# The convolution group's GLU projection inside the attention stream of a hybrid decoder block

## The reference

```python
h = rms_norm(x, norm_mix[l])
z = h @ w_in[l]                                               # (B,T,IN_WIDTH)
q, kc, vc, ksl, vsl, kw, vw, g, u = jnp.split(z, splits, axis=-1)
...
o_cmp, p_cmp = compressed_attention(q, k_cmp, v_cmp, slopes)
# selected-block branch (top-k blocks from compressed scores)
sel_idx = select_blocks(p_cmp, T)
o_slc = selected_attention(q, rms_norm(ksl.reshape(kv_shape), k_norm_slc[l]), vsl.reshape(kv_shape), sel_idx, slopes)
# sliding-window branch
o_win = window_attention(q, rms_norm(kw.reshape(kv_shape), k_norm_win[l]), vw.reshape(kv_shape), slopes)
gates = jax.nn.sigmoid(g + gate_b[l]).reshape(B, T, G, Hg, N_BRANCH)
o_nsa = (gates[..., 0:1] * o_cmp + gates[..., 1:2] * o_slc + gates[..., 2:3] * o_win).reshape(B, T, NSA_WIDTH)
# Conformer convolution group
o_conv = conformer_conv(u, conv_w[l], conv_b[l], conv_ln_g[l], conv_ln_b[l])
x = x + jnp.concatenate([o_nsa, o_conv], axis=-1) @ w_out[l]
```

## Time and profile before

| | us |
|---|---|
| median of 3 runs | 2215.68 (2213.09 to 2215.70) |
| the profiled execution | 2215.39 |
| its span, slowest core (3) | 2214.3 |
| spans of the eight cores | 2204.7 to 2214.3 |
| TensorE busy, core 3 | 1892.4 |
| VectorE, ScalarE, GpSimd busy | 993.2, 496.4, 126.6 |

### The profile page before, as it was taken

How to read it: one execution, slowest core, us unless ns; L and a number is a source line. 1 busy time by engine, 2 the same in 40 slices (tenths; PEclk the granted TensorE clock), 3 DMA queues, 4 the chain that set the end, 5 groups by cost and what they waited for, 6 DMA issues and landing times.

```text
span 2214.3 us, 30692 instructions; the slowest of 8 cores (2204.7 to 2214.3 us)
## 1 busy us (share of the span) xinstructions
PE 1892.4 (85%) x11010; PEld 999.1 (45%) x11010; DVE 993.2 (45%) x1726; ACT 496.4 (22%) x951; POOL 126.6 (6%) x129
## 2 busy tenths in 40 slices
PE   4898879976666779929957679999999999999999
PEld 2555534443334534318843344444444444444444
DVE  3565591014666666843257634144144144134134
ACT  3222221014776852230033210000000000000000
POOL 1100100100000000001000000010010010010000
PEclk9999999976878999959969879999999999999999
DMA  9621963653210200029622202852852852862853
GB/s 217 121 77 24 110 72 44 66 68 55 40 30 1 40 1 1 1 82 206 95 39 39 38 7 33 113 80 37 113 79 38 112 81 38 111 82 38 110 77 152
DMA packets 187219, 153.20 MB, mean 69 GB/s; under 512 B 12992, under 2 KB 176448, under 8 KB 182720
## 3 DMA queue, kind: packets, MB, share of 16 engines
q0 software_dynamic: 173968, 107.13, 38.1%
q1 hardware_dynamic: 13104, 44.12, 6.4%
HBM read 249.83 MB, written 8.52 MB: 117 GB/s over the span
## 4 chain that ended last, share of the span: by engine, by line
PE 78%; DVE 11%; issue 3%; another core or an unknown queue 3%; ACT 3%; POOL 1%; DMA 0%; DVEq 0%; ACTq 0%; SPq 0%; POOLq 0%
PE bank L1139 14%; PE bank L1156 14%; PE bank L1141 14%; PE bank L470 13%; PE bank L1020 5%; PE bank L949 5%; PE bank L730 3%; PE bank L709 2%; PE bank L477 2%; DVE arena L421 2%; DVE arena L457 1%; PE bank L417 1%; PE bank L1106 1%; PE bank L647 1%
## 5 line engine op out<-in xcount | busy, mean ns | idle before, releaser
L470 PE MATMUL bank<-arena 128*128 128x512 bf16 (+2 forms) x1728 | 329.9, 349 | 10.2 <-DVE arena L614 6.7
L1139 PE MATMUL bank<-arena 128*128 128x512 bf16 x1408 | 319.8, 380 | 0.0
L1141 PE MATMUL bank<-arena 128*128 128x512 bf16 x1408 | 318.3, 379 | 0.0
L1144 DVE TENSOR_TENSOR arena<-bank,arena 128x512 bf16<-128x512 f32 x88 | 60.8, 691 | 548.4 <-PE bank L1139 442.8
L1156 PE MATMUL bank<-arena 128*128 128x512 bf16 x1408 | 305.7, 379 | 0.0
L1159 DVE TENSOR_TENSOR arena<-bank,arena 128x512 f32<-128x512 f32 x352 | 242.4, 691 | 60.7 <-DVE arena L1159 37.7
L1143 ACT ACTIVATE arena<-bank 128x512 bf16<-128x512 f32 x88 | 52.5, 597 | 824.0 <-PE bank L1139 810.8
L470 PEld LDWEIGHTS bank<-arena 128*128 128x128 bf16 x1728 | 152.1, 99 | 177.8 <-issue 16.1
L719 ACT ACTIVATE arena<-bank,arena 128x512 bf16<-128x512 f32 (+2 forms) x504 | 213.5, 530 | 59.5 <-PE bank L709 24.2
L1139 PEld LDWEIGHTS bank<-arena 128*128 128x128 bf16 x1408 | 138.2, 98 | 167.0 <-issue 1.9
L1141 PEld LDWEIGHTS bank<-arena 128*128 128x128 bf16 x1408 | 137.8, 98 | 166.1
(11 more groups left out here) (124 smaller groups left out, 1326.3 us busy)
## 6 DMA issues: line engine op xcount, KB each, us to landing
arena<-xc SPq DMA_DIRECT2D x24, 1024.0 KB, 9.3
arena<-w_gate POOLq DMA_DIRECT2D x22, 1024.0 KB, 14.7
arena<-w_up POOLq DMA_DIRECT2D x22, 1024.0 KB, 16.7
arena<-w_down POOLq DMA_DIRECT2D x22, 1024.0 KB, 13.4
arena<-w_in POOLq DMA_DIRECT2D x18, 1024.0 KB, 13.2
arena<-w_out POOLq DMA_DIRECT2D x8, 1024.0 KB, 32.6
y<-arena SPq DMA_DIRECT2D x8, 1024.0 KB, 3.9
arena<-sel SPq DMA_DIRECT2D x4, 1024.0 KB, 8.1
```

The source lines that it names most:

```text
L470: op(PE, lambda: nc.tensor.matmul(bank[psi][:, 0:n], lhsT=wt[:, kc, cc * 128:(cc + 1) * 128], rhs=actT[:, kc, t0:t0 + n], start=(kc == 0), ...
L1139: op(PE, lambda: nc.tensor.matmul(bank[pg][:, :], lhsT=wgt[:, kc, cc * 128:(cc + 1) * 128], rhs=h3T[:, kc, tc * 512:(tc + 1) * 512], start ...
L1141: op(PE, lambda: nc.tensor.matmul(bank[pu][:, :], lhsT=wut[:, kc, cc * 128:(cc + 1) * 128], rhs=h3T[:, kc, tc * 512:(tc + 1) * 512], start ...
```

## The change

The stage `u_proj` ahead of the compression is gone. Its matmuls become a generator of single matmuls (three segments of 352 columns instead of 32 + 512 + 512), which a new `run_stream` uses as filler. While the program is built, every engine has a clock (`Eng.clk`): each instruction advances it by `_cost`, and its result is ready after `LATENCY`. At each step `run_stream` takes what can start first on TensorE: a transpose, the next score (up to six tiles ahead; seven `Pt` buffers) or the next value products; if by the clocks TensorE would wait, it issues one matmul of the filler first. A wait on an engine's own earlier result is not charged (`if tok.eng is not self`), and a DMA is charged 3 us.

Banks 6 and 7 now belong to the projection; scores and transposes share banks 0 and 1. The groups no longer overlap: cmp, win and sel of one group, then the next; mask, accumulator and importances are single, the latter two tracked by quarter. The heads' outputs overwrite the queries (`catA = qnT`). The sigmoid becomes 0.5 (tanh(x/2) + 1), its factor 0.5 going into the convolution weights, and `CHUNK` is 256 in head 0 and 512 in the others. The normalised inputs stay in one tile `hT` until the attention ends. The memory stage gets a loop of its own, in the same order as before.

```diff
-CHUNK = [128, 256] + [512] * 6
+CHUNK = [256] + [512] * 7
+NPTS = 7
...
+LATENCY = {"pe": 250.0, "act": 280.0, "dve": 200.0, "pool": 200.0, "sp": 0.0}
+
+def _cost(name, ins):
...
+    if name == "pe":
+        return max(n, 64) / 2.4
+    if name == "act":
...
+        return n / 1.2 + fixed
...
+        return n / (1.92 if small else 0.96) + 68.0
...
+        if tok.eng is not self:
+            self.at = max(self.at, tok.t)
...
+        self.clk = max(self.clk, self.at) + _cost(self.name, ins)
+        self.at = 0.0
+        return Tok(self.sem, self.cnt, self, self.clk + LATENCY[self.name])
...
+        tok = Tok(owner.dsem, owner.dcnt, None, Q.clk + 3000.0)
...
-        for j4 in range(4):
-            wa, wab = wget()
-            wbt, wbb = wget()
...
-                    pa = proj_fm(wa, wab, cc, actT, actb, t0, n)
-                    pb = proj_fm(wbt, wbb, cc, actT, actb, t0, n)
...
-        rot_S = Rot([0, 1, 6])
+        rot_S = Rot([0, 1])
...
-                        at(4, tr)
+                        when([ocbb[oj]], tr)
...
+                        for kc in range(16):
+                            op(PE, lambda: nc.tensor.matmul(bank[6][:, 0:352], lhsT=wbt[:, kc, cc * 128:(cc + 1) * 128], rhs=hT[:, kc, c0:c0 + 352], start=(kc == 0), stop=(kc == 15)), r=[wbb] + hseg[seg], w=[bankb[6]])
+                            yield True
+                        j = rot_sg.next()
+                        op(ACT, lambda: nc.scalar.activation(out=sg[j][:, 0:352], in_=bank[6][:, 0:352], func=AF.Tanh, scale=0.5), r=[bankb[6]], w=[sgb[j]])
...
+                        op(DVE, lambda: nc.vector.scalar_tensor_tensor(out=hglu[:, ch, c0:c0 + 352], in0=sg[j][:, 0:352], scalar=1.0, in1=bank[7][:, 0:352], op0=ALU.add, op1=ALU.mult), r=[bankb[7], sgb[j]], pw=[hglub[ch]])
...
+            while nxt or pend or later:
+                cands = []
+                for k, (bufs, fn) in enumerate(later):
+                    cands.append((max(ready(bufs), when_s()), 0, k))
+                if nxt is not None and len(pend) < L:
+                    cands.append((when_s(), 1, 0))
+                if pend:
+                    pvf, pj, Ob = pend[0]
+                    cands.append((max(ready([Ptb[pj]]), vacant([bankb[o] for o in Ob])), 2, 0))
+                t, kind, k = min(cands, key=lambda c: (max(c[0], PE.clk), c[1]))
+                if t > PE.clk and next(filler, self) is not self:
+                    continue
...
-        run_stream([cmp_jobs(0), win_jobs(0), cmp_jobs(1), sel_jobs(0), win_jobs(1), cmp_jobs(2), sel_jobs(1), win_jobs(2), cmp_jobs(3), sel_jobs(2), win_jobs(3), sel_jobs(3)], 3)
...
+        run_stream(all_jobs(), NPTS - 1, u_proj())
```

More of the change, by code:

```diff
@@ L492, in build @@
         op(POOL, lambda: nc.gpsimd.memset(Vaug[:, :, :, :], 1.0), w=Vaugb)
-        hTs = [self.tile(P1, f"hT{c}", [128, 16, 512], BF16) for c in range(2)]
+        hT = self.tile(P1, "hT", [128, 16, 1056], BF16)
         hTb = [self.buf(f"hT{c}") for c in range(2)]
-        htail = self.tile(P1, "htail", [128, 16, 32], BF16)
         htailb = self.buf("htail")
@@ L686, in build @@
         rot_ocb = Rot([0, 1])
-        imp = [self.tile(AT, f"imp{j}", [128, 4, 32], F32) for j in range(2)]
-        impb = [self.buf(f"imp{j}") for j in range(2)]
+        imp = self.tile(AT, "imp", [128, 4, 32], F32)
+        impb = [self.buf(f"imp{j}") for j in range(4)]
         sc2 = self.tile(AT, "sc2", [128, 4, 32], F32)
@@ new lines, in run_stream, with when_s @@
+        def run_stream(jobs, L, filler):
+            jobs = iter(jobs)
+            filler = iter(filler)
+            pend = []
+            nxt = next(jobs, None)
+            sync_clocks()
+            def when_s():
+                return vacant([bankb[rot_S.peek()]])
+            while nxt or pend or later:
[10 more added lines that the diff above has]
+                    continue
+                if kind == 0:
+                    later.pop(k)[1]()
+                elif kind == 1:
+                    sc, pvf, Ob = nxt
+                    pend.append((pvf, sc(), Ob))
+                    nxt = next(jobs, None)
+                else:
+                    pend.pop(0)
+                    pvf(pj)
+            for _ in filler:
+                pass
@@ L895, in build @@
+        P1.close()
+        self.free(hTb + [htailb, gtmpb])
         A.close()
[L896 removed]
+        self.free([b for l in KnTb for b in l] + Vaugb + [gatesb, kcmpb, vcaugb, cbb])
         catB = self.tile(CT, "catB", [128, 8, TQ], BF16, hi=True)
@@ L1096, in build @@
         pend_tr = []
-        run_stream([jobs], 2)
+        mp = []
+        for sc, pvf in jobs:
+            mp.append((pvf, sc()))
+            if len(mp) > 2:
+                f, pj = mp.pop(0)
+                f(pj)
+        while mp:
+            f, pj = mp.pop(0)
+            f(pj)
         while pend_tr:
```

194 lines of the change are left out of this document (100 added, 94 removed).

## The result

The changed kernel takes 2111.1 us (median of four runs, 2110.5 to 2111.75) where the kernel before takes 2215.7: a ratio of 0.953, 95% interval 0.951 to 0.955. The forecast was 2092 us, with a range from 2053 to 2122: right in sign, inside the range, 19 us short. Two of the chains that it priced came as forecast; the pace of a selected tile did not. Times and ratios are of executions in which all eight cores had their usual granted clock; some had one die at a lower one and are left out. The profiled execution took 2111.0 us; its slowest core is core 4 (span 2109.9 us), and the lines of after are that core's.

What follows compares the result with a forecast made beforehand. No engine was full in the attention; each waited in turn. TensorE's 246.8 us of work plus stalls and ends made a 313.9 us stream, replacing 129.1 + 308.0: 123.2 us saved from 2215.4, giving 2092 us, range 2053 to 2122.

Steps and rivals of the forecast that it cites:

- the clock's rival: Compressed heads: the clock falls to 1.2 GHz each time, 25 us more, total 2117 us; chance 0.22.
- (d): Start, first score to first value product: 5.1 us of wait on the bias table's load stay, plus 1.0 for the clock.
- (a): Compressed heads, first value product to selection transposes: VectorE's chain takes 14.2 us a group, stalling TensorE 19.9 us in all.
- (b): Mask's trip through memory, selection transposes to first selected value product: 17.9 to 21.3 us a group, 13.3 us stall in all.
- (c): Output transposes wait for each head's finish: 0.3 us each for 14 heads with filler, 4.2 us.
- (e): End: last two heads without filler at 9.8 us each, 19.6 us, plus 4.0 from last score to last transpose.
- the price of a selected tile: Selected heads on two score banks: score, exponential and two hand-overs make 1.28 us for two tiles, 0.64 a tile.
- a sign of error: Among the signs that would show the forecast wrong: tiles pacing at over 0.7 us.
- The model right: Terms (a) to (c) vanish as VectorE and DMAs run ahead during filler: stream 276.5 us, total 2055; chance 0.12.
- Table swaps: ScalarE: each tanh between exponentials brings two table loads, 61.6 us in all, total 2154; chance 0.03.
- Two banks as the bound: Late refills leave one tile in flight at 1.28 us, total 2296; slower than before from 1.06 us a tile; chance 0.03.
- The lower clock: Current limit takes the die to 13/16 clock: the stream's 260.6 us of TensorE work become 320.7, total 2152; chance 0.02.

Runs made afterwards that it cites:

- the changed prices: Changed kernel with three planner prices set to its trace (VectorE waits for its own results, 0.057 us more for wide f32 instructions, 5 us per DMA): 0.953 of before.
- two experiments: Kernel before with two score banks instead of three: 1.013 of before. Changed kernel with three score banks, projection halves sharing one bank: 0.977 of before.
- halves: Changed kernel with the mask's second half read back without waiting for the first half: 2107.2 us, and 2109.4 in a second run.
- finish: Changed kernel leaving out three of the four weighted sums at the end of each selected head: 0.951 of before.
- order: Changed kernel with the next group's compressed heads placed one by one between this group's selected heads: 0.952 of before.
- two runs: The changed kernel (2111.1 us), and it with three score banks, both projection banks and three value-product banks instead of four (0.960 of before).

## Why the prediction was right, and where it was short

The forecast saved 123.2 us and 104.4 came. The 18.8 us between them are 12.7 in the stream's own sum (326.6 against 313.9), 2.5 at the projection's place (the way from the gate logits to the compression shrank from 142.0 to 15.4 us, 126.6 and not 129.1), 1.9 behind the stream, 1.2 ahead of the gate logits on the core that is now the slowest, and half a microsecond of rounding. By the number alone 2111 lies outside the forecast's own band (2070 to 2105) and next to the clock's rival (2117); it is the granted clock that decides against that one. And the sum's error is smaller than its terms': the start came 3.8 us shorter and the compressed heads 3.7 us longer.

**The start (d), 10.5 us: 6.7.** The bias table's wait is 3.4 us and the clock is back 4.5 us after the first score.

**Compressed heads (a), 14.2 us each: 14.8 to 15.6.** Right. VectorE's chain sets the stretch; counted from the starts of TensorE's instructions at the prices of the earlier trace rows, TensorE stalls 23.4 us there, where 19.9 were forecast.

**The mask's trip (b), 17.9, 21.2, 18.0, 21.3 us: 17.9, 20.3, 17.7, 20.4.** Right.

**Output transposes (c), 4.2 us, and the last two heads with the end (e), 19.6 + 4.0: the mis-sized terms.** TensorE's stalls ahead of output transposes are 0.5 us in all while the projection lasts. It stalls some 14 us in the selected heads up to there, 11 to 12 of it ahead of value products. The last two heads and the end take 28.6 us, not 23.6. Together that is some 15 us, the last stretch of the table. The step that failed is the price of a selected tile, 0.64 us "with two banks". It added the parts of a bank's round and left out TensorE's order: the next score stands behind value products that wait for VectorE. The trace has 0.75 us a tile and 2.1 us at each change of head. With the changed prices, which place scores and products in another order, the selected stretches took 170.3 us on two banks, 2 us more than the forecast's 168.2: the order is what it left out. The row of before that was to confirm it, 9.2 us from transposes to transposes, begins where such a pause ends. Over a full period, from the score that ends one pause to the score that ends the next, the kernel before takes 11.1 us (core 3, in order of time):

```profile
793.88 0.38 PE L709 MATMUL bank<-arena 128*128 128x512 bf16 x1
...
804.99 0.38 PE L709 MATMUL bank<-arena 128*128 128x512 bf16 x1
```

The forecast named this itself as a sign of error: tiles at over 0.7 us.

**What the sum was made of.** The forecast added TensorE's 246.8 us of work to its stalls, as if the work set the length. As bookkeeping that holds: up to the last head but one the trace has some 246 us of work and 52 of stalls in 298, counted from start to start at the prices of the earlier trace rows. As a cause it doesn't. With 113.7 us of that work taken away, the stalls grow by as much and the stream stays. What sets it with two score banks is the round of tile, exponential, mask and value product, in the order that TensorE's queue gives it; the projection only takes what is idle. That the sum came near I put down to the planner, which had laid the work where the idle time was, so that each stall was counted once.

**The price that the forecast missed.** It never charged the change for the bank that the projection takes from the scores: 30 us, by two experiments. It appears in the forecast only as "9.2 becomes 9.8" in the last two heads. The sum was not 30 us short by that, since it prices the new stream from its parts and not from the old one's length. The wider exponentials, which it put at nothing, gave 5 back.

**Rivals.** The model right (2055): no, both chains are there. The clock falls in the compressed heads: the granted clock is 1.00 there, where it was 0.58. Table swaps: one load. Two banks as the bound: the rival that named the right resource, at a pace that did not come; 0.75 us a tile is under its 1.06. The lower clock: the stream ran at 0.98 with TensorE busy 285 of 327 us (core 4), all eight cores at work. The Trainium skill ("TensorE: Matmul & The Clock Gate", Part 1) budgets 13/16 of the clock for that; no stretch of this trace shows it.

**What stays open.** With two banks four edits on four different waits (prices, halves, finish, order) moved the stream by 2 to 3.3 us each. With the changed prices that is 13 us won in the selected heads and 11 lost ahead of them. The number of banks and the order in TensorE's queue were shown to matter; which of the links in a tile's round gives way first was not separated. No run has the order that wins in the selected heads without its loss elsewhere and with two banks.

## What to carry to other kernels

Work put into an engine's idle time is free only as long as that engine is not the bound, and its busy share doesn't tell: TensorE at 95% gave the same head time as at 72%. The order in an in-order queue is a price too: the same selected tiles on the same banks took 13 us less in another order. Ask what the moved work takes with it; here a PSUM bank cost 30 us and the matmuls almost nothing. To price a pace, measure over a full period, from one start to the next, and take the filler out once to see what is left.

## What the runs showed of the hardware

- Without the projection the granted clock in the first compressed heads is 0.65 (core 3), with it 1.00, and the stretch is no longer (14.6 against 14.8 us): a low clock cost nothing where another engine sets the time.
- ScalarE's 512-wide exponentials last 0.69 us each by the trace, yet with three banks the scores that wait for them stand 0.57 us apart: successive ones overlap, and the duration is not the pace.
- A 32 KB store took 1.4 to 2.2 us with no weight block of its core in flight (48 stores in two runs) and 4.1 to 6.3 us beside the 1 MB blocks (16 stores). The mask's trip behind such a store (VectorE's copy to GpSimd's first multiply) took 19 to 27 us, where it had taken 15 to 18.
